# Token-block loads and sink logits as indirect transfers with one row index per partition (one-core hybrid diffusion backbone)

## The chip, the core and the metric

The kernel runs on one core of one Trainium2 chip. A core has the tensor engine (PE in the profile, its weight loads PEld), the vector engine (DVE), the scalar engine (ACT), GpSimd (POOL) and the sync engine (SP), and 16 DMA engines that move data between the device memory and the on-chip memory of 128 partitions. The metric is the device time of one execution in microseconds; of several executions the median is taken.

## What is computed

Two layers run over 768 tokens of width 1024 in float32: 256 context tokens and 512 latent tokens. Cut to what matters here:

```
for l in range(2):
    mod   = silu(c)  @ w_mod[l] + b_mod[l]            # six vectors of shift, scale and gate
    h     = modulate(rms_norm(x, norm_mix_w[l]), mod[0], mod[1])
    mixed = [HGRN2 recurrence, windowed attention with swa_sink[l], neighbourhood attention](h @ w_in[l])
    x     = x + mod[2] * (mixed @ w_out[l])
    h     = modulate(rms_norm(x, norm_ffn_w[l]), mod[3], mod[4])
    q     = h @ peer_wq[l];  scores against 2 x 128 subkeys, top 16 of 16 x 16 per head, 8 heads
    y     = sum over the retrieved experts e of  g_e * gelu(u_e . h) * v_e      # 16384 experts
    x     = x + mod[5] * y
return rms_norm(x_latent, final_norm_w)
```

The context tokens take part in the first layer's feed-forward step and are only read in the second. `swa_sink` has shape (2, 6): one logit for each layer and head, which joins the softmax of the windowed attention.

## The kernel before

The 768 tokens are six blocks of 128 (`NB = 6`, blocks 0 and 1 are context). The residual stream lives between the stages in the device memory, in the tensor `xs` of 768 rows and 1024 columns. The on-chip memory holds a ring of four weight slots of 1 MB, a large `arena` whose places are used anew by each stage, and the pair buffers `hS`, `wS` and `gS_` of the expert products.

SP streams the weights and nothing else: 40 tiles of 1 MB (modulation, input and output projections) for each layer and, for each expert pass, 8 tiles of `wq` and 128 tiles of experts, each 1 MB, into the ring, as slots come free (`stream`, L260).

The work is cut into stages. At the end of each, `stage_end` (L243) lets PE, DVE, ACT and POOL drain, add one to `stage_end` and wait for all four. The stages of a layer are mod, norm, projA, hg, readout, projB, rope, attn, mixT and mix. Then come the expert passes over two blocks each (three in the first layer, two in the second), with the stages pnorm, topk, gbuild, gemm and pres. In gemm all 16384 experts are applied densely to 256 tokens, 128 experts to a step, each product split in high and low parts: PE runs 24 matmuls of 256 columns (L847) and 12 of 512 (L862) in a step.

POOL issues every DMA that isn't a weight stream, in program order:

- At the start (L296 to L298) it loads the constants `ident`, `iota`, `c` and `lb`, and then for each layer the six token blocks (L311) and nine small things (L313 to L319), the sink logits among them: one DMA that repeats the 24 bytes of `swa_sink[l]` over 128 partitions. DVE waits for the four constants (its L1359, before L1360) to compute silu(c); PE's first matmul (L637) waits for that. DVE waits for the nine small loads with `layer_in` at the end of the mod stage.
- At the end of mod (L321, L322) POOL waits for DVE's gates and stores them.
- `load_pass` (L376 to L378) loads the two token blocks of an expert pass from `xs` into `xl`. ACT waits for both in pnorm (L1046) before its first instruction there (L901). For the first pass of a layer it is called at the start of the stage pnorm (L380), with the subkeys behind it (L384). For the others it is called in the gemm stage of the pass before.
- In gemm, POOL waits until all but eight of the 128 expert steps have their gates (`gfull`, L422). Then it issues the gate vector (L425), the two blocks again for the residual (`xr`, L427 and L428), and, where another pass follows, the subkeys (L430) and `load_pass`. DVE needs `gbP` and `xr` in the stage pres (L1706 to L1709), after which POOL stores the two blocks (L436).

POOL computes as well: the bias mask (L348), a product in topk (L397) and the scaled one-hot rows in gbuild (L412, L413).

## Time and profile before

| | |
|---|---|
| three runs | 7344.88, 7344.93 and 7348.73 us, median 7344.93 |
| profiled execution, first to last instruction | 7343.4 us |
| PE, share of the span | 85% (6235.5 us) |
| DVE | 56% (4125.4 us) |
| ACT | 33% (2451.6 us) |
| POOL | 12% (847.7 us) |
| mean granted clock of TensorE | 0.867 |
| DMA | 859.86 MB, mean 117 GB/s |

The profiled execution's own device time isn't given apart from its span. The span is 1.5 us below the median of the runs, and that difference is taken as what lies around it.

The page lists busy time by engine; below it the trace gives instructions in order of time with the idle time before them and what ended it, groups of instructions by line, waits, and the issue and landing of each DMA. For a DMA that POOL issues, the time on the engine is only the issue; "landing" is counted from the start of the issue to the last increment of its semaphore. The granted clock is a share of full speed, 2.4 GHz: 1.00 is that level and 0.50 the other, 1.2 GHz.

### The profile page before, as it was taken

To read this page: it belongs to the slowest core of one execution; us is meant where nothing else is said; L and a number is where in the kernel's file an instruction comes from. 1 tells how busy PE (TensorE), PEld (TensorE's weight loads), DVE (VectorE), ACT (ScalarE), POOL (GpSimd) and SP (SyncE) were. 2 spreads that over 40 slices of the span, in tenths; PEclk is the share of its full clock that TensorE was granted. 3 is DMA by queue.
4 is the path that set the end of the run, shared out by engine and by line. 5 is a ranking of instruction groups with operands and counts; after the bars stand their busy time and mean duration, and the time that the engine had idled before them with its cause. 6 is when DMAs were issued, how large, how long until landed. Compare 5 with 4: busy or idle time off the path is not lost. (4 is left out here: it accounts for less than half of the span.)

```text
span 7343.4 us, 99482 instructions
## 1 busy us (share of the span) xinstructions
PE 6235.5 (85%) x34486; PEld 5371.5 (73%) x34486; DVE 4125.4 (56%) x7294; ACT 2451.6 (33%) x3904; POOL 847.7 (12%) x917
## 2 busy tenths in 40 slices
PE   8659997599995899985999986599858999669997
PEld 3546776499984799974899845468647999559997
DVE  1561335955558755569555515623296555785554
ACT  1111321244441344432444412212114444224444
POOL 0000020600003400006000000001142000060000
PEclk9768558799997999997999997685679999889999
DMA  5001012055551255540455540010213555305554
GB/s 194 18 0 43 9 49 95 0 183 188 185 200 46 87 188 188 184 156 0 177 184 187 197 170 18 6 38 22 81 38 115 188 185 186 129 18 188 188 184 171
DMA packets 127361, 859.86 MB, mean 117 GB/s; under 512 B 15544, under 2 KB 15592, under 8 KB 29320
## 3 DMA queue, kind: packets, MB, share of 16 engines
q1 hardware_dynamic: 109440, 796.97, 29.9%
q0 software_dynamic: 17808, 61.46, 2.4%
q8 instruction: 63, 1.03, 0.1%
q14 instruction: 50, 0.41, 0.0%
HBM read 845.74 MB, written 12.62 MB: 117 GB/s over the span
## 5 line engine op out<-in xcount | busy, mean ns | idle before, releaser
L847 PEld LDWEIGHTS PS<-hS,wS 128*128 128x128 f32 x15360 | 1929.9, 192 | 68.0 <-issue 11.5
L847 PE MATMUL PS<-hS,wS 128*128 128x256 f32 x15360 | 1947.2, 283 | 16.6 <-ACT wS L1085 16.6
L862 PE MATMUL PS<-wS,gS_ 128*128 128x512 f32 x7680 | 1863.1, 391 | 8.7 <-ACT wS L1101 8.7
L862 PEld LDWEIGHTS PS<-wS,gS_ 128*128 128x128 f32 x7680 | 1401.3, 188 | 275.9 <-issue 8.2
L1673 DVE TENSOR_TENSOR wS<-ring,wS 128x1024 fp32r<-128x1024 f32 x640 | 784.0, 1225 | 926.8 <-ACT wS L1085 926.8
L1085 ACT ACTIVATE wS<-ring 128x1024 fp32r<-128x1024 f32 x640 | 678.1, 1060 | 1002.6 <-PE PS L847 1001.7
L1691 DVE TENSOR_TENSOR wS<-ring,wS 128x1024 fp32r<-128x1024 f32 x640 | 784.2, 1225 | 343.5 <-ACT wS L1101 343.5
L1101 ACT ACTIVATE wS<-ring 128x1024 fp32r<-128x1024 f32 x640 | 667.9, 1044 | 7.3 <-PE PS L862 7.3
L1659 DVE TENSOR_TENSOR wS<-iota,arena 128x512 fp32r<-128x512 f32 x640 | 647.2, 1087 | 0.6
L824 PE MATMUL PS<-wS,arena 128*128 128x128 f32 x2560 | 466.7, 340 | 203.9 <-POOL arena L413 198.1
L824 PEld LDWEIGHTS PS<-wS,arena 128*128 128x128 f32 x2560 | 400.0, 239 | 271.4 <-ACT arena L1070 184.4
L1097 ACT ACTIVATE gS_<-arena 128x256 fp32r<-128x256 f32 x640 | 267.3, 418 | 859.3 <-DVE arena L1683 859.3
L413 POOL TENSOR_TENSOR arena<-wS,arena 128x512 f32<-128x512 f32 x320 | 474.0, 1481 | 65.5 <-DVE wS L1659 65.5
L1687 DVE TENSOR_TENSOR gS_<-arena,gS_ 128x256 fp32r<-128x256 f32 x640 | 272.4, 426 | 309.5 <-ACT gS_ L1097 309.5
L425 POOL DMA_DIRECT2D arena<-gates x5 | 3.0, 594 | 3396.5 <-DVE arena L1683 3396.5
L1070 ACT ACTIVATE arena<-PS 128x512 f32 x320 | 191.1, 597 | 596.7 <-PE PS L824 596.7
L793 PE MATMUL PS<-arena,ring 128*128 128x256 f32 x1280 | 303.4, 393 | 44.6 <-DVEq L246 30.7
L793 PEld LDWEIGHTS PS<-arena,ring 128*128 128x128 f32 x1280 | 246.1, 197 | 91.7 <-issue 58.8
L542 PE MATMUL PS<-ring,arena 128*128 128x256 f32 x1152 | 255.6, 384 | 51.6 <-DVEq L246 48.6
L542 PEld LDWEIGHTS PS<-ring,arena 128*128 128x128 f32 x1152 | 220.8, 193 | 86.4 <-DVEq L246 48.9
L584 PE MATMUL PS<-arena 64*128 (+2 forms) x576 | 270.6, 640 | 4.0 <-DVE arena L1180 4.0
L1683 DVE TENSOR_TENSOR arena<-arena 128x256 f32<-128x256 f32 x640 | 267.3, 418 | 5.6 <-ACT arena L1094 5.6
(247 smaller groups left out, 5335.4 us busy)
## 6 DMA issues: line engine op xcount, KB each, us to landing
ring<-in_experts SPq DMA_DIRECT2D x640, 1024.0 KB, 4.8
ring<-in_wcat SPq DMA_DIRECT2D x80, 1024.0 KB, 4.8
ring<-in_wq SPq DMA_DIRECT2D x40, 1024.0 KB, 4.8
arena<-xs POOLq DMA_DIRECT2D x34, 512.0 KB, 6.9
arena<-in_rpb POOLq DMA_DIRECT2D x96, 128.0 KB, 2.6
xs<-arena POOLq DMA_DIRECT2D x20, 512.0 KB, 2.9
arena<-in_subk POOLq DMA_DIRECT2D x5, 1024.0 KB, 11.2
arena<-gates POOLq DMA_DIRECT2D x9, 512.0 KB, 4.7
```

Of the source, the lines that this page charges most:

```text
L413: pool.tensor_tensor(oneA[g % 2], oneR[g].bitcast(F32), arena[:, bass.ds(i * (4 * GD) + (KT0 + 2 * PASS + 4 * g), 4)].unsqueeze(2) .broadc ...
L542: mm = pe.matmul(bank[n % 4][:, 0:TW], hT[:, k, part * P:(part + 1) * P], w[:, k, :], start=(k == 0), stop=(k == KD - 1))
L793: mm = pe.matmul(bank[n % 4][:, 0:PASS], w[:, m, k, :], hP[:, k, :], start=(k == 0), stop=(k == KD - 1))
L824: mm = pe.matmul(bank[4 + g][:, q * P:(q + 1) * P], oneA[g % 2][:, q, :], oneB[g][:, q, :].bitcast(F32), start=True, stop=True)
L847: mm = pe.matmul(bank[c % 2][:, 0:PASS], u[:, k, :], hS[:, h, k, :], start=(part == 0 and k == 0), stop=(part == 2 and k == KD - 1))
L862: mm = pe.matmul(bank[4 + 2 * tb + h], gS_[:, 2 * (c % 2) + g, tb * P:(tb + 1) * P], wS[:, 2 + v, 512 * h:512 * h + 512], start=(start and ...
L1085: act.activation(wS[:, 0, :], ring[:, sl, 0:D], ACT.Copy).then_inc(s["u_hi"], 1)
L1101: act.activation(wS[:, 2, :], ring[:, c, D:2 * D], ACT.Copy).then_inc(s["v_hi"], 1)
L1659: last = dve.tensor_tensor(dst[g], iota[:, :].unsqueeze(1).broadcast_to([P, 4, P]), at.unsqueeze(2).broadcast_to([P, 4, P]), ALU.is_equal)
L1673: dve.tensor_tensor(wS[:, 1, :], ring[:, c % SLOTS, 0:D], wS[:, 0, :].bitcast(F32), ALU.subtract).then_inc(s["u_lo"], 1)
L1687: dve.tensor_tensor(gS_[:, 2 * (c % 2) + 1, :], gel[2 + c % 2], gS_[:, 2 * (c % 2), :].bitcast(F32), ALU.subtract).then_inc(s["gated"], 1)
L1691: dve.tensor_tensor(wS[:, 3, :], ring[:, c, D:2 * D], wS[:, 2, :].bitcast(F32), ALU.subtract).then_inc(s["slot_free"], 1)
```

## The change

A new tensor `rowid` of 18 unsigned words in each partition is filled at the program's start by 18 `iota` instructions on POOL. Column b (0 to 5) holds `b * 128 + partition`, the row of `xs` that belongs to the partition in block b. Columns 6 to 17 hold one number in all partitions, the flat position of one sink logit. POOL waits for all 18 before it goes on.

The loads of `xl` (`load_pass`) and `xr` become indirect transfers (`rows_of`): each partition's row of 4 KB is fetched from the row of `xs` that `rowid` names. That is 20 DMAs, the same bytes to the same places. The one DMA of the sink logits in each layer becomes six, one for each head, each bringing 4 bytes to each of 128 partitions (`sinks_of`); they stand behind the other eight small loads, and the count that DVE waits for rises from 144 to 224 (14 times 16). The loads of `xin`, `xw` and `xf`, all stores, the subkeys and the weights stay as they are.

`rowid` stands ahead of `arena`, which is 32 words shorter. In the built programs `arena` begins 96 bytes later than before, and `hS`, `wS` and `gS_` 32 bytes earlier; the ring and the small tensors ahead of it stay.

```diff
...
         modp = sb("modp", [P, 4 * KD, 2])
         modA = sb("modA", [P, 2, KD, 2])
         small = sb("small", [P, 160])
-        ARENA = 35264
+        rowid = sb("rowid", [P, NB + DEPTH * SWA_H], U32)
+        ARENA = 35232
         arena = sb("arena", [P, ARENA])
 
         hS = sb("hS", [P, 2, KD, PASS], F32R)
...
             "sub_in", "s_done", "s_used", "gexp", "gready", "sel_ready", "selT_done", "one_ready",
             "rows_ready", "eq_want", "eq_done", "u_hi", "u_lo", "v_hi", "h_hi", "gfull", "g_hi", "down_done",
             "one_used", "g_used", "hu_done", "gelu_done", "gated", "fin_ready", "fin_out0", "fin_out1",
-            "nrm_in")}
+            "nrm_in", "ids_ready")}
         w_ready = [sem(f"w_ready{i}") for i in range(SLOTS)]
         block = ctx.enter_context(nc.Block())
         N_STAGED = 4
...
                 pool.dma_start(dst, src).then_inc(s["consts_in"], 16)
 
             pool.nop().then_inc(s["bias_ready"], 1)
+            for b in range(NB):
+                pool.iota(rowid[:, b:b + 1], [[0, 1]], base=b * P, channel_multiplier=1).then_inc(s["ids_ready"], 1)
+            for i in range(DEPTH * SWA_H):
+                pool.iota(rowid[:, NB + i:NB + i + 1], [[0, 1]], base=i, channel_multiplier=0).then_inc(s["ids_ready"], 1)
+            pool.wait_ge(s["ids_ready"], NB + DEPTH * SWA_H)
+
+            def rows_of(dst, b, signal):
+
+                pool.indirect_dma_start(out=dst, out_offset=None, in_=d["xs"][:, :],
+                                        in_offset=bass.IndirectOffsetOnAxis(ap=rowid[:, b:b + 1], axis=0)
+                                        ).then_inc(signal, 16)
+
+            def sinks_of(l):
+
+                flat = d["sink"].rearrange("l (h o) -> (l h) o", o=1)
+                for h in range(SWA_H):
+                    at = NB + l * SWA_H + h
+                    pool.indirect_dma_start(out=sink[:, h:h + 1], out_offset=None, in_=flat,
+                                            in_offset=bass.IndirectOffsetOnAxis(ap=rowid[:, at:at + 1], axis=0)
+                                            ).then_inc(s["layer_in"], 16)
+
             for dst, src in ((ident[:, :], d["ident"]), (iota[:, :], d["iota"]), (c0, d["c"]), (lbx, d["lb"])):
                 const(dst, src)
 
...
 
                 for dst, src in ((bT, d["bT"][l]), (nw, d["nw"][l]),
                                  (brow[0:2, :], d["bgate"][l:l + 1, :].broadcast_to([2, 2048])),
-                                 (sink, d["sink"][l:l + 1, :].broadcast_to([P, SWA_H])),
                                  (arena[:, CST:CST + 512], d["masks"]), (arena[:, CST + 512:CST + 768], d["rope"]),
                                  (arena[:, CST + 768:CST + 1024], d["swam"]), (natm, d["natm"]),
                                  (hnw, d["hnw"][l:l + 1, :].broadcast_to([P, 256]))):
                     pool.dma_start(dst, src).then_inc(s["layer_in"], 16)
+                sinks_of(l)
 
                 pool.wait_ge(s["mod_done"], l + 1)
                 pool.dma_start(d["gates"][l], grow[0:2, :]).then_inc(s["gates_out"], 16)
...
 
                 def load_pass(b0):
                     for i in range(2):
-                        pool.dma_start(xl[:, i, :], d["xs"][(b0 + i) * P:(b0 + i + 1) * P, :]).then_inc(s["xp_in"], 16)
+                        rows_of(xl[:, i, :], b0 + i, s["xp_in"])
 
                 load_pass(passes_of(l)[0])
                 for pn, b0 in enumerate(passes_of(l)):
...
                     pool.dma_start(gbP, d["gates"][l, st:st + 1, D:2 * D].broadcast_to([P, D])
                                    ).then_inc(s["gate_in"], 16)
                     for i in range(2):
-                        pool.dma_start(xr[:, i, :], d["xs"][(b0 + i) * P:(b0 + i + 1) * P, :]).then_inc(s["gate_in"], 16)
+                        rows_of(xr[:, i, :], b0 + i, s["gate_in"])
                     if b0 + 2 < NB:
                         pool.dma_start(subk, d["subk"][l]).then_inc(s["sub_in"], 16)
                         load_pass(b0 + 2)
...
                         dve.tensor_copy(arena[0:2, bass.ds(i * 2048 + (ROWS + 1024 * r), 1024)], PS[r][0:2, :]
                                         ).then_inc(s["row_taken"], 1)
                 dve.wait_ge(s["row_taken"], MOD_TILES // SLOTS * (l + 1) + 2)
-                dve.wait_ge(s["layer_in"], 144 * (l + 1))
+                dve.wait_ge(s["layer_in"], 224 * (l + 1))
 
                 dve.wait_ge(s["modT_done"], l + 1)
                 link(dve.tensor_tensor(modp[:, :, :], bank[4][:, 0:64].rearrange("p (n s) -> p n s", s=2), bT, ALU.add))
```

POOL at the start of the program, before (from the branch into the engine's block to the first token loads):

```order
L287 UNCONDITIONAL_BRANCH
L293 DMA ident<-in_ident 128x128
L293 DMA iota<-in_iota 128x128
L293 DMA small<-in_c 128x16
L293 DMA small<-in_lb 128x8
L311 DMA arena<-in_ctx 128x1024 x2
L311 DMA arena<-in_x 128x1024 x4
```

and now:

```order
L288 UNCONDITIONAL_BRANCH
L298 ISA
L298 IOTA rowid 128x1 x6
L300 IOTA rowid 128x1 x12
L294 DMA ident<-in_ident 128x128
L294 DMA iota<-in_iota 128x128
L294 DMA small<-in_c 128x16
L294 DMA small<-in_lb 128x8
L333 DMA arena<-in_ctx 128x1024 x2
L333 DMA arena<-in_x 128x1024 x4
```

The ISA row stands for the reload of POOL's instruction library and the 18 iotas for the row numbers; both now stand ahead of the four constants. Before, the reload stood ahead of the first mask sum in the stage attn (L348).

POOL from the stage mix to the first product of topk in the first layer, before:

```order
L370 DMA xs<-arena 128x1024 x6
L378 DMA arena<-xs 128x1024 x2
L384 DMA arena<-in_subk 128x2048
L397 TENSOR_TENSOR arena<-arena 128x1024 x6
L413 TENSOR_TENSOR arena<-wS,arena 128x512 x2
```

and now:

```order
L392 DMA xs<-arena 128x1024 x6
L305 DMA arena<-xs,rowid 128x1024 x2
L406 DMA arena<-in_subk 128x2048
L419 TENSOR_TENSOR arena<-arena 128x1024 x6
L435 TENSOR_TENSOR arena<-wS,arena 128x512 x2
```

The two block loads stand at the same place, ahead of the subkeys, and read `rowid` besides `xs`.

POOL at the end of the first expert pass (gemm and pres), before:

```order
L425 DMA arena<-gates 128x1024
L428 DMA arena<-xs 128x1024 x2
L430 DMA arena<-in_subk 128x2048
L378 DMA arena<-xs 128x1024 x2
L436 DMA xs<-arena 128x1024 x2
```

and now:

```order
L447 DMA arena<-gates 128x1024
L305 DMA arena<-xs,rowid 128x1024 x2
L452 DMA arena<-in_subk 128x2048
L305 DMA arena<-xs,rowid 128x1024 x2
L458 DMA xs<-arena 128x1024 x2
```

Four of the six loads are indirect now; their order is the same.

## Rows read from the trace of the kernel before

**Rows 1.** The page: the span, and from its part 5 the costliest matmul groups.
```profile
span 7343.4 us, 99482 instructions
...
L847 PE MATMUL PS<-hS,wS 128*128 128x256 f32 x15360 | 1947.2, 283 | 16.6 <-ACT wS L1085 16.6
L862 PE MATMUL PS<-wS,gS_ 128*128 128x512 f32 x7680 | 1863.1, 391 | 8.7 <-ACT wS L1101 8.7
```

**Rows 2.** Instructions in order of time, POOL, 0 to 60 us: start, us, engine line op [idle before].
```profile
0.38 0.10 POOL L1809 MEMSET const-float32-0.0<- 128x1 f32 x1 [0.38 <-issue]
0.42 0.10 POOL L1809 MEMSET const-float32-1.0<- 128x1 f32 x1
...
3.25 0.53 POOL L293 DMA_DIRECT2D small<-in_lb  x1
```

**Rows 3.** The same, DVE, 0 to 175 us.
```profile
9.85 0.21 DVE L1360 TENSOR_SCALAR sT<-small 128x16 f32<-128x16 f32 x1 [9.85 <-DMA small<-in_lb]
...
42.44 1.21 DVE L1381 COPY arena<-PS 2x1024 f32 x1 [12.60 <-PE PS L637]
56.26 1.21 DVE L1381 COPY arena<-PS 2x1024 f32 x1 [12.61 <-PE PS L637]
...
101.23 0.23 DVE L1387 TENSOR_TENSOR modp<-PS,small 128x64 f32<-128x64 f32 x1 [2.33 <-PE PS L644]
```

**Rows 4.** The same, PE, 0 to 175 us.
```profile
12.63 84.91 PE L637 MATMUL PS<-ring,sT 128*2 128x256 f32 x384 [12.63 <-DVEq L1373]
```

**Rows 5.** Groups of instructions of POOL: mean ns after the busy time.
```profile
L412 POOL TENSOR_TENSOR small<-small 128x1 f32<-128x1 f32 x310 | 138.3, 446 | 49.3 <-POOL arena L413 15.3 <-PE PS L824 5.6 <-DVE wS L1659 3.1
L397 POOL TENSOR_TENSOR arena<-arena 128x1024 f32<-128x1024 f32 x30 | 80.6, 2712 | 609.0 <-DVE arena L1297 609.0
...
L378 POOL DMA_DIRECT2D arena<-xs x10 | 5.3, 530 | 20.1 <-POOLq L246 20.1
```

**Rows 6.** Line L348, 700 to 712 us: counts, ns min/median/max, start.
```profile
L348 POOLq MODIFY_POOL_CONFIG  x2: 42/42/42, 708.2 to 708.3; - x2
L348 POOL TENSOR_TENSOR arena<-arena x1: 1254/1254/1254, 710.3 to 710.3; 128x512 f32<-128x512 f32 x1
```

**Rows 7.** Instructions in order of time, POOL, 480 to 760 us.
```profile
710.31 1.25 POOL L348 TENSOR_TENSOR arena<-arena 128x512 f32<-128x512 f32 x1 [2.06 <-DMA arena<-in_rpb]
...
714.71 1.25 POOL L348 TENSOR_TENSOR arena<-arena 128x512 f32<-128x512 f32 x1 [2.14 <-DMA arena<-in_rpb]
```

**Rows 8.** The same, POOL, 1160 to 1205 us.
```profile
1173.74 1.06 POOL L378 DMA_DIRECT2D arena<-xs  x2 [10.15 <-POOLq L246]
```

**Rows 9.** The same, ACT, 1160 to 1205 us.
```profile
1179.79 1.06 ACT L901 ACTIVATE arena<-arena 128x1024 f32<-128x1024 f32 x1 [104.15 <-DMA arena<-xs]
```

**Rows 10.** The same, POOL, 5272 to 5300 us.
```profile
5282.55 1.06 POOL L378 DMA_DIRECT2D arena<-xs  x2 [9.94 <-POOLq L246]
```

**Rows 11.** The same, ACT, 5272 to 5300 us.
```profile
5288.20 1.06 ACT L901 ACTIVATE arena<-arena 128x1024 f32<-128x1024 f32 x1 [77.20 <-DMA arena<-xs]
```

**Rows 12.** Landing of the ten loads of L378 in us.
```profile
DMA to landing us min/median/max: 3.9/14.0/15.3
```

**Rows 13.** DMA, 1173 to 1176 us: queues, MB, share of the 16 engines.
```profile
q1 hardware_dynamic: 144, 0.98, 77.7%
```

**Rows 14.** Instructions in order of time, POOL, 2137 to 2195 us.
```profile
2138.14 0.59 POOL L425 DMA_DIRECT2D arena<-gates  x1 [680.37 <-DVE arena L1683]
2138.72 1.05 POOL L428 DMA_DIRECT2D arena<-xs  x2
...
2140.28 1.05 POOL L378 DMA_DIRECT2D arena<-xs  x2
```

**Rows 15.** Landing of the ten loads of L428 in us.
```profile
DMA to landing us min/median/max: 5.3/6.3/7.7
```

**Rows 16.** Instructions in order of time, DVE, 2183 to 2215 us.
```profile
2186.78 1.22 DVE L1708 TENSOR_TENSOR arena<-PS,arena 128x1024 f32<-128x1024 f32 x1 [1.98 <-ACTq L246]
```

**Rows 17.** Waits of POOL: us in total, times, longest us.
```profile
POOL gates L322 <- DVE arena L1393: 178.0, 2, 93.3
```

## The prediction, made before the changed kernel ran

> **What bounds the kernel now.** I read the page first, then, for each place that the change touches, the instructions in order of time on POOL and on the engine that waits for it, then the landings of POOL's DMAs. The page gives a span of 7343.4 us and the two matmul groups of the expert steps, 1947.2 and 1863.1 us busy: these 3810 us are the body of the kernel, and nothing of the change stands in a step [rows 1]. So the change can act only where somebody waits for POOL or for one of its loads, or where it slows somebody at a distance. The trace shows three kinds of such places.
>
> The start: POOL issues the four constants from 1.5 us, and the last, `lb`, is issued at 3.25 us [rows 2]. DVE's first instruction waits for it until 9.85 us [rows 3], and PE's first matmul follows at 12.63 us and then runs for 84.91 us without a pause [rows 4]. DVE takes a result every 13.82 us (56.26 less 42.44), and had waited for PE all the time between: PE sets the pace of this stage, the weights are there [rows 3]. A later start of PE is a later end of the stage, one for one.
>
> The first pass of each layer: POOL issues the two loads of `xl` at 1173.74 us and ACT starts at 1179.79 us, 6.05 us later [rows 8, 9]. In the second layer it is 5282.55 to 5288.20, 5.65 us [rows 10, 11]. Every engine stands still meanwhile.
>
> The last eight steps of a gemm: POOL starts to issue at 2138.14 us and DVE wants the first of it at 2186.78 us. That is 48.64 us of cover [rows 14, 16].
>
> **The 18 iotas at the start: 4.4 us, on the path.** No iota is in the trace. Below, it can't be less than the spacing of two memsets of the same shape, 0.04 us (0.42 less 0.38): 18 x 0.04 = 0.7 us [rows 2]. Above, I take POOL's 128x1 sum, 446 ns, which reads two operands that an iota hasn't: 18 x 0.446 = 8.0 us [rows 5]. An iota writes one column as the memset does, but its function has to be called as the sum's is. I take the middle, 0.245 us: 18 x 0.245 = 4.4 us. The wait for all 18 stands behind them in the same queue; I give it 0.1 us, an allowance.
>
> **The library reload: 1.0 us, on the path.** The change moves the reload of POOL's library from the attention to the start. Before, two pool configurations stand at 708.2 us and the product after them starts at 710.31, 2.1 us after the first [rows 6]. It waited 2.06 us there for a DMA, and the next such product, with no reload ahead of it, waited 2.14 [rows 7]. So the reload was hidden and costs between 0 and 2.1 us; I take the middle, 1.0. At the start nothing hides it, since `lb`'s load is behind it. Nothing comes back in the attention, where the DMA is waited for anyway.
>
> The Trainium skill, "GPSIMD Engine Reference", section Instruction dispatch, has it otherwise: the first call to freshly loaded code pays about 6 us that no instruction shows. The row doesn't agree, since the product ran 2.1 us after the configurations; by the page the sum would be 5.0 us higher, and the verdict the same.
>
> `lb`'s own landing, 6.6 us after its issue today (9.85 less 3.25), was already beside the ring's stream, and I leave it [rows 2, 3]. Together the start costs 4.4 + 0.1 + 1.0 = 5.5 us, between 0.7 and 10.2 (8.0 + 0.1 + 2.1).
>
> **The sinks: nothing.** Five more DMAs in each layer, and six of them indirect, stand last among the small loads. Behind them POOL waits for DVE's gates, 178.0 us in two waits, so up to 93.3 and at least 84.7 us [rows 17]. Even at 7 us each, six take 42. DVE needs all of them only at 101.23 us [rows 3]. The cover is gone at 14 us each.
>
> **The indirect issue itself.** Call x the time that POOL needs to issue one load of 128 rows by index. The direct one takes 0.530 us [rows 5]. An indirect one does the same and reads 128 numbers besides, so it can't be less. Above, the longest group of POOL instructions has a mean of 2.712 us [rows 5]. Nearest is a direct issue plus one small reading instruction: 0.530 + 0.446 = 0.98 us. I take x = 1.0.
>
> **The first pass of each layer: 1.0 us in all.** The fastest of the ten loads of this line landed 3.9 us after its issue began, 3.4 after it ended [rows 12]. Two indirect issues in a row and one such landing give 2x + 3.4: at x = 1.0 that is 5.4 us, less than the 6.05 and 5.65 of now, because now both compete with the ring, whose stream held 77.7% of the DMA engines' work in the first 3 us [rows 13]. So part of the longer issue lies beside traffic that was awaited anyway. I count half of the added issue, 0.5 us a layer, 1.0 us in all. At x = 2.712 the formula gives 8.8 us: 2.8 and 3.2 more, 6.0 together. The lower end is nothing. The subkeys are issued 1 us later and aren't needed before topk.
>
> The Trainium skill, "DMA: Bandwidth & Descriptors", section Anatomy of one DMA, calls descriptor generation "small, variable" beside a fixed 2.0 us for a transfer. By that x would stay at 0.53 and this term would be 0; the 3.4 us above, with 512 KB to move, don't speak against it.
>
> **The gemm stages: nothing.** There are 20 indirect loads, and 16 of them are issued here. In the three passes that another follows in their layer, four stand behind the gate vector and beside the subkeys: 4x + 0.59 + 0.53 = 5.1 us of issue against 48.64 us of cover [rows 14, 16]. `xr`'s own landing, 7.7 us at most today, stands inside it too [rows 15]. In the last pass of a layer there are two. What is queued behind them on POOL is only the end of the stage. The cover is gone at x = (48.64 - 1.12) / 4 = 11.9 us. The bytes and the rows of 4 KB are the same, so the ring sees what it sees now.
>
> **The sum.** 5.5 + 1.0 = 6.5 us: a span of 7349.9 us. The profiled execution's span lies 1.5 us below the median of the runs, 7344.93; so the time is 7351.4 us, 0.09% more. The bounds of the terms give 0.7 to 16.2 us more, 7345.6 to 7361.1. A measurement of this kernel can tell about 0.2%, 14.7 us, from no change.
>
> **The rivals.**
>
> *POOL walks the index list (slower).* The rows of a DMA are shared by 16 engines. If POOL reads the indices for each of them by a step of its own, at the price of its smallest reading instruction, x = 16 x 0.446 = 7.1 us [rows 5]. The first passes then take 2 x 7.1 + 3.4 = 17.6 us instead of 6.05 and 5.65: 11.55 + 11.95 = 23.5 us. With the start that is 29 us more: 7374 us. The gemms still hide it (28.4 + 1.1 = 29.5 us). It decides from x = 3.6 on: 2 x 3.6 + 3.4 = 10.6 in each of two layers is 21.2, less the 11.7 of now 9.5, and 9.5 + 5.5 passes 14.7. For it: nothing in this trace reads a list on POOL. Against it: a direct load writes entries for the same 128 rows in 0.53 us [rows 5]. I give it 15 in 100.
>
> The Trainium skill's "GPSIMD Engine Reference", section Performance pitfalls for Q7 kernels, has a rule of this kind: about 102 cycles for each read command, "e.g. one per gather index", that don't overlap. With 128 in a row at the 1.2 GHz of its specifications this is an estimate of 10.9 us for x, and 7389 us. No row here shows such reads.
>
> *The layout (either sign).* `hS`, `wS` and `gS_` start 32 bytes earlier, `arena` 96 later. If an engine or a DMA depends on where in a line of memory a row starts, all 640 steps feel it: 0.4% of 3810 us is 15 us [rows 1]. For it: these four are nearly all that the steps touch. Against it: no row compares two placements. 7366 or 7336 us; 3 in 100 on each side.
>
> *A shorter way (faster).* The rows of an indirect load may be given to the DMA engines otherwise and land sooner. All of the wait that it could take away is 6.05 + 5.65 = 11.7 us less the issue, so this alone can't pass 0.2%. Only together with another granted clock after one of the waits could it. I give 2 in 100, at 7328 us.
>
> *It does nothing:* if x = 0.53 and an iota costs as a memset, 0.7 us more. This is the lower end of my forecast, not a case of its own.
>
> **How the numbers follow.** Forecast 0.77, walk 0.15, layout 0.06, shorter way 0.02. The bounds of the forecast reach over 14.7 us at their end (16.2), for which I move 0.02 to slower. Faster: 0.03 + 0.02 = 0.05. Slower: 0.15 + 0.03 + 0.02 = 0.20. Within 0.2%: 0.75. The likeliest case gives 7351.4 us. The range begins at 7343.0, somewhat below the lower bound, and ends at 7376, so that the walk as priced is held; outside are the layout, the shorter way, a walk at a longer step and some of the forecast's own error.
>
> **What would show it.** POOL's rows at the start: 18 iotas of about 0.25 us and `lb` issued near 8.8 us instead of 3.25; PE's first matmul near 18.1 instead of 12.63 us, and the mod stage later by the same. The indirect loads near 1.0 us of issue each, and 6 to 7 us from the first of them to ACT in the first passes. In gemm, ACT, DVE and PE keep their steps while POOL issues, and the stage pres waits for nothing of POOL's. I am wrong if `lb`'s landing doesn't delay PE, if an indirect issue takes over 3.6 us, or if L847 and L862 (now under other line numbers) change their means.

## The result and the profile after

| | before | after |
|---|---|---|
| runs of the comparison | 18 | 18 |
| median, us | 7346.11 | 7361.57 |
| lowest and highest, us | 7340.90, 7349.15 | 7355.06, 7369.85 |
| profiled execution, span, us | 7343.4 | 7358.8 |
| mean granted clock of TensorE | 0.867 | 0.865 |

The ratio is 1.0022 with a 95% interval of 1.0015 to 1.0029: 15.5 us slower. That is a difference, and a hair over the 0.2% that I called the edge of what can be told. The time is within the range of the prediction (7343.0 to 7376.0), but 9 us of the 15.5 are not in its sum. Three executions of the later comparisons took 13574, 18489 and 27077 us at a granted clock far from the others' 0.866; they move a median by 0.4 us at most and are left out of the ratios.

The page of after, the lines that answer to [rows 1]:

```profile
span 7358.8 us, 99500 instructions
PE 6240.5 (85%) x34486; PEld 5375.6 (73%) x34486; DVE 4126.8 (56%) x7294; ACT 2453.8 (33%) x3904; POOL 872.7 (12%) x945
L869 PE MATMUL PS<-hS,wS 128*128 128x256 f32 x15360 | 1947.5, 283 | 16.6 <-ACT wS L1107 16.6
L884 PE MATMUL PS<-wS,gS_ 128*128 128x512 f32 x7680 | 1863.2, 391 | 8.7 <-ACT wS L1123 8.7
```

The body of the kernel is as it was: 1947.5 and 1863.2 us against 1947.2 and 1863.1. So the time came in at the edges, and I followed them in order. POOL at the start, which answers to [rows 2] (start, duration, engine, line, operation):

```profile
1.06 0.50 POOL L298 IOTA rowid<- 128x1 uint32 x6 [0.47 <-POOLq L1831]
1.52 0.94 POOL L300 IOTA rowid<- 128x1 uint32 x12
2.77 0.70 POOL L294 DMA_DIRECT2D ident<-in_ident  x1 [0.31 <-POOL rowid L300]
...
4.54 0.53 POOL L294 DMA_DIRECT2D small<-in_lb  x1
...
12.77 1.03 POOL L314 DMA_INDIRECT small<-in_sink,rowid  x1 [0.30 <-issue]
14.11 0.98 POOL L314 DMA_INDIRECT small<-in_sink,rowid  x1 [0.30 <-issue]
...
19.13 0.94 POOL L314 DMA_INDIRECT small<-in_sink,rowid  x1 [0.30 <-issue]
```

All 18 iotas take 1.40 us (2.46 less 1.06), and `lb` is issued at 4.54 instead of 3.25 us. The six sink loads are issued by 20.07 us. PE in order of time, 0 to 180 us and 4205 to 4345 us, which answers to [rows 4]:

```profile
13.44 18.84 PE L659 MATMUL PS<-ring,sT 128*2 128x256 f32 x80 [13.44 <-DVEq L1395]
35.94 67.46 PE L659 MATMUL PS<-ring,sT 128*2 128x256 f32 x304 [3.65 <-DMA ring<-in_wcat]
...
4230.75 26.52 PE L659 MATMUL PS<-ring,sT 128*2 128x256 f32 x112 [9.32 <-ACTq L247]
4260.91 58.87 PE L659 MATMUL PS<-ring,sT 128*2 128x256 f32 x272 [3.64 <-DMA ring<-in_wcat]
```

Here is what I hadn't foreseen. PE ran 384 matmuls without a pause in [rows 4]. Now it stands still in both layers, for 3.65 and 3.64 us, and what it waits for is no load of POOL's but a weight tile of the ring (16 matmuls use one up). The DMA view of 20 to 34 us, in 40 slices of 0.35 us (busy tenths of the DMA engines, then GB/s), first before the change and then after it:

```profile
DMA  9999225899999999999998999999999999999998
GB/s 410 404 329 49 82 105 176 339 410 468 439 421 421 456 369 386 392 375 416 468 410 374 445 398 421 445 398 468 421 398 421 398 421 445 468 421 398 351 398 351
```

```profile
DMA  9999999989899989111101001003432275585789
GB/s 374 410 387 281 363 375 416 380 322 415 351 445 369 381 328 352 59 59 47 25 0 47 24 24 24 24 23 95 164 141 117 117 258 234 211 304 234 304 351 398
```

From 25.6 us on, traffic falls from some 400 to between 0 and 59 GB/s for about 3.9 us (11 slices) and takes another 4 us to come back. The digits are as low: the DMA engines are busy for less than a fifth of each slice. Before the change there was a small hollow of the same kind, four slices long, near 21 us. The weight tiles of the ring come in through the same stretch. Their number, size and median time to landing there, before and after:

```profile
ring<-in_wcat SPq DMA_DIRECT2D x4, 1024.0 KB, 7.1
```

```profile
ring<-in_wcat SPq DMA_DIRECT2D x4, 1024.0 KB, 12.3
```

The mod stage ends later by the wait and a little more. The granted clock in windows of PE from 28.90 us on (columns: us, PE busy and matmuls, clock as a share of 2.4 GHz, DMA share, GB/s):

```profile
28.90:32.28 3.38, 3.38 (x16) 1.00 0.38 148
32.28:35.94 3.66, 0.01 (x2) 1.00 0.87 360
35.94:37.94 2.00, 2.00 (x7) 0.72 1.00 422
37.94:39.94 2.00, 2.00 (x6) 0.50 0.97 406
39.94:41.94 2.00, 2.00 (x11) 0.93 0.61 258
```

After 3.66 us of standing still the clock falls to its lower level (0.50 is 1.2 GHz) for some 3 us. There eight matmuls start 0.427 us apart instead of 0.216, which costs 1.7 us. The stage begins with such a slow stretch in every kernel, 7 to 13 matmuls long; here it is seven, before it was nine, which gives 0.4 us back. All 384 matmuls take 86.30 us (18.84 + 67.46) instead of 84.91 [rows 4]. So the stage ends 0.81 (PE's start, 13.44 less 12.63) + 3.65 + 1.39 = 5.85 us late; DVE's row at its end, at 101.23 us in [rows 3], reads:

```profile
107.10 0.23 DVE L1409 TENSOR_TENSOR modp<-PS,small 128x64 f32<-128x64 f32 x1 [2.34 <-PE PS L666]
```

107.10 less 101.23 is 5.87 us. In the second layer the stage grows by 3.6 us once more. There the wait is as long, and no slow stretch follows it:

```profile
4260.91:4319.78 58.87, 58.87 (x272) 1.00 0.85 309
```

The first passes, POOL and ACT in order of time, and then the group of all twenty indirect block loads with their landing. They answer to [rows 8 to 12]:

```profile
1181.57 1.00 POOL L305 DMA_INDIRECT arena<-xs,rowid  x1 [10.32 <-POOLq L247]
1182.88 0.97 POOL L305 DMA_INDIRECT arena<-xs,rowid  x1 [0.30 <-issue]
```

```profile
1188.56 1.06 ACT L923 ACTIVATE arena<-arena 128x1024 f32<-128x1024 f32 x1 [104.34 <-DMA arena<-xs,rowid]
...
5299.17 1.06 ACT L923 ACTIVATE arena<-arena 128x1024 f32<-128x1024 f32 x1 [76.79 <-DMA arena<-xs,rowid]
```

```profile
L305 POOL DMA_INDIRECT arena<-xs,rowid x20: 937/968/2060, 1181.6 to 7275.5; - x20
...
DMA to landing us min/median/max: 3.9/8.2/14.8
```

ACT starts 6.99 us after the first issue in layer 1 (before: 6.05) and 6.07 us after it in layer 2 (5293.10; before: 5.65). An issue takes 0.97 us.

A table of how much later than before each mark comes, in us, in the profiled executions of after and of three experiments, shows where the difference grows. The last column is the end:

| | end of mod 1 | first pass 1 | end of layer 1 | end of mod 2 | first pass 2 | last gemm starts | end |
|---|---|---|---|---|---|---|---|
| after | 5.87 | 8.77 | 7.01 | 10.73 | 10.97 | 14.14 | 15.4 |
| sinks direct | 2.10 | 3.52 | 3.25 | 3.19 | 2.60 | 3.45 | 4.7 |
| blocks direct | 5.68 | 6.74 | 6.95 | 9.48 | 7.89 | 10.11 | 10.0 |
| iotas only | 1.64 | -0.57 | -2.50 | -3.34 | -3.91 | -0.26 | 1.8 |

Steps of 1 to 4 us also stand between marks where nothing was changed: a single execution can't tell less than that. The medians have to.

### The profile page after: what moved, and what is told of

The parts are those of the page before. It is cut to its first block and busy times, and to the rows that moved or that the text cites. A ratio compares the mean times of both kernels' runs of the same rounds, so it can differ in the third digit from the quotient of the medians.

```text
span 7358.8 us, 99500 instructions
## 1 busy us (share of the span) xinstructions
PE 6240.5 (85%) x34486; PEld 5375.6 (73%) x34486; DVE 4126.8 (56%) x7294; ACT 2453.8 (33%) x3904; POOL 872.7 (12%) x945
## 3 DMA queue, kind: packets, MB, share of 16 engines
q8 instruction: 63, 1.03, 0.1%
## 5 line engine op out<-in xcount | busy, mean ns | idle before, releaser
L869 PE MATMUL PS<-hS,wS 128*128 128x256 f32 x15360 | 1947.5, 283 | 16.6 <-ACT wS L1107 16.6
L884 PE MATMUL PS<-wS,gS_ 128*128 128x512 f32 x7680 | 1863.2, 391 | 8.7 <-ACT wS L1123 8.7
L564 PE MATMUL PS<-ring,arena 128*128 128x256 f32 x1152 | 255.7, 384 | 51.6 <-DVEq L247 48.6
```

The costliest lines, as they stand in the source:

```text
L564: mm = pe.matmul(bank[n % 4][:, 0:TW], hT[:, k, part * P:(part + 1) * P], w[:, k, :], start=(k == 0), stop=(k == KD - 1))
L869: mm = pe.matmul(bank[c % 2][:, 0:PASS], u[:, k, :], hS[:, h, k, :], start=(part == 0 and k == 0), stop=(part == 2 and k == KD - 1))
L884: mm = pe.matmul(bank[4 + 2 * tb + h], gS_[:, 2 * (c % 2) + g, tb * P:(tb + 1) * P], wS[:, 2 + v, 512 * h:512 * h + 512], start=(start and ...
```

## The experiments

Twelve runs were made, of eleven kernels (11 is the kernel of 8). The theories carry letters in the expectations: A, the sink loads hold up the ring, with A1, because a table of twelve rows is spread over too few DMA engines; P, because there are so many small pieces; and R, because all pieces read one address (P and R together are A2 in the first expectations, and Q is the width of a piece). B: the block loads cost it. C: the later start. D: the layout. All diffs are against the changed kernel unless said otherwise.

**1. Sinks as one direct load again, all else as changed.**

```
                                  (brow[0:2, :], d["bgate"][l:l + 1, :].broadcast_to([2, 2048])),
+                                 (sink, d["sink"][l:l + 1, :].broadcast_to([P, SWA_H])),
...
-                sinks_of(l)
...
-                dve.wait_ge(s["layer_in"], 224 * (l + 1))
+                dve.wait_ge(s["layer_in"], 144 * (l + 1))
```

> The change with the sinks loaded as before, one direct DMA a layer at its old place; iotas and the 20 indirect block loads stay. Theory A (the sinks' small indirect transfers hold back a weight tile in each mod stage, 5.5 us of drift in the first layer and 3.8 in the second): PE shows no wait for a tile in either mod stage, the end of mod lies within 1.5 us of before plus the start's 0.8, and the time is 5 to 7 us over before, some 9 us under the change. Rival B (the block loads cost the time, by their longer issue and later landing in the first pass of each layer and at the gemm ends): 12 to 15 us over before remain. Rival C (the later start alone shifts the weight stream against the token loads and makes the stall): the stall is still there.

Measured: 7351.26 us against 7346.68 before, ratio 1.0007 (0.9998 to 1.0016). PE in order of time:

```profile
13.99 85.64 PE L659 MATMUL PS<-ring,sT 128*2 128x256 f32 x384 [13.99 <-DVEq L1395]
...
4227.17 85.08 PE L659 MATMUL PS<-ring,sT 128*2 128x256 f32 x384 [9.49 <-ACTq L247]
```

The wait is gone in both layers, and with it some two thirds of the loss (15.5 less 4.6 us by the medians).

**2. Block loads direct again, sinks still indirect.**

```
-                        rows_of(xl[:, i, :], b0 + i, s["xp_in"])
+                        pool.dma_start(xl[:, i, :], d["xs"][(b0 + i) * P:(b0 + i + 1) * P, :]).then_inc(s["xp_in"], 16)
...
-                        rows_of(xr[:, i, :], b0 + i, s["gate_in"])
+                        pool.dma_start(xr[:, i, :], d["xs"][(b0 + i) * P:(b0 + i + 1) * P, :]).then_inc(s["gate_in"], 16)
```

> The change with xl and xr loaded directly as before; the iotas and the twelve indirect sink loads stay. Theory A: both stalls of PE for a weight tile stay, 9 to 10 us over before. Rival B: under 4 us over before. If the two parts add up, this difference and that of the run with direct sinks sum to the 15.5 us of the change plus about 1 us for the iotas, counted twice.

Measured: 7355.46 us, 8.8 more than before, ratio 1.0014 (1.0005 to 1.0023). PE:

```profile
13.53 18.75 PE L659 MATMUL PS<-ring,sT 128*2 128x256 f32 x80 [13.53 <-DVEq L1395]
35.75 67.46 PE L659 MATMUL PS<-ring,sT 128*2 128x256 f32 x304 [3.48 <-DMA ring<-in_wcat]
```

The wait belongs to the sinks, not to the blocks.

**3. The sinks' table padded from 12 to 16 rows.** The Trainium skill, "DMA: Bandwidth & Descriptors", section "Why a DMA increments its semaphore by 16 and not by 1", states that a DMA uses the largest number of engines up to 16 that divides the outer sizes of both sides. By that a table of 12 rows and a tile of 128 partitions would go over 4 engines, one of 16 rows over all 16, if the rule holds for the table of an indirect load.

```
-                flat = d["sink"].rearrange("l (h o) -> (l h) o", o=1)
+                flat = d["sink"]
...
-    A["sink"], A["hnw"] = a["swa_sink"], a["hgrn_norm_w"]
+    A["sink"], A["hnw"] = np.concatenate([a["swa_sink"].reshape(12, 1), np.zeros((4, 1), np.float32)]), a["hgrn_norm_w"]
```

> The change with the table of sink logits padded from 12 to 16 rows, four of them zero and never read; same indices, same 768 packets of 4 bytes a layer. Theory A1 (the number of rows of the source, 12, lets only 4 of the 16 DMA engines carry the sinks, as 4 is the largest number up to 16 that divides 12 and 128; those four hold back their share of a weight tile): with 16 rows all 16 engines share the packets, 8 each instead of 32 for a DMA, and the stall falls to a quarter or less: under 1.5 us in each mod stage, 6 to 8 us over before. Rival A2 (what counts is the total of small packets or that all read one address): the stall stays at 3.7 us of PE's wait and more.

Measured: 7358.38 us against 7346.68, ratio 1.0015 (1.0006 to 1.0025). PE:

```profile
31.04 3.61 PE L659 MATMUL PS<-ring,sT 128*2 128x256 f32 x16 [1.92 <-DMA ring<-in_wcat]
35.38 65.77 PE L659 MATMUL PS<-ring,sT 128*2 128x256 f32 x304 [0.72 <-DMA ring<-in_wcat]
...
4257.22 58.87 PE L659 MATMUL PS<-ring,sT 128*2 128x256 f32 x272 [2.93 <-DMA ring<-in_wcat]
```

5.6 us of waiting instead of 7.3. The wait shrinks and stays: the number of rows is at most a part of it. The trace doesn't name the engine of a packet, so no run here shows the rule, and on how many engines either table went stays open. In both kernels, and in 8 and 9, a layer's six sink loads show 96 packets of 32 bytes, eight pieces in each.

**4. Six direct loads of 4 bytes, repeated over the partitions, in place of the six indirect ones.**

```
-                    pool.indirect_dma_start(out=sink[:, h:h + 1], out_offset=None, in_=flat,
...
+                    pool.dma_start(sink[:, h:h + 1], flat[at - NB:at - NB + 1, :].broadcast_to([P, 1])).then_inc(s["layer_in"], 16)
```

> The change with each of the six sink loads of a layer as a direct DMA that repeats one 4-byte logit over 128 partitions; the same number of DMAs and packets, no index. Theory A1 (few engines because of the 12-row source): a direct DMA is spread over all 16 engines, the stall is gone, 5 to 8 us over before. Rival A2 (small packets or one address as such): the stall stays. The issue falls from 0.94 to about 0.54 us each.

Measured: one run, 7360.4 us, span 7358.1. PE, and the DMA view of 20 to 34 us:

```profile
32.64 70.92 PE L657 MATMUL PS<-ring,sT 128*2 128x256 f32 x320 [2.21 <-DMA ring<-in_wcat]
```

```profile
DMA  9999999940000000001111223569999999999999
GB/s 433 410 406 285 351 375 357 311 107 12 0 1 0 0 1 24 24 24 47 47 47 47 94 71 117 211 258 375 421 445 445 398 421 445 421 421 445 445 398 421
```

The wait is there without any index, in layer 2 too (3.34 us), and so is the hollow in the traffic. It begins earlier, as the loads are issued earlier (0.57 us each). What stalls the ring isn't the indirect transfer as such: the change had replaced one small load by six.

**5. Only the iotas and the layout: no indirect load at all.** The edits of experiments 1 and 2 together.

> The change without any indirect transfer: only rowid, its 18 iotas and the wait for them at the start; block loads and sinks as before. What it costs is the later start alone: PE's first matmul 0.8 to 1.4 us later (13.44 and 13.99 us were seen against 12.63), the end of mod 1 to 2 us later, no wait of PE for a weight tile. Theory A: 1 to 3 us over before. Rival C (the shift of the start makes the stalls): 8 us and more. Rival D (the 32 and 96 bytes by which the buffers moved cost in every expert step): 3 us and more, growing evenly over the passes.

Measured: 7346.79 us against 7345.12, ratio 1.0001 (0.9992 to 1.0010), PE without a pause (13.41 us, 384 matmuls in 85.76 us). The later start makes no stall, so C falls. The time alone, with an interval of -6 to 7 us, can't exclude the 3 us of D. The matmul groups speak against it: that of 256 columns took 1949.0 us here and 1949.5 in experiment 12, which has the old layout. The medians are 1.7 us apart.

**6. The six sink loads issued after the mod stage.**

```
                 end(f"mod{l}")
+                sinks_of(l)
                 end(f"norm{l}")
...
-                dve.wait_ge(s["layer_in"], 224 * (l + 1))
+                dve.wait_ge(s["layer_in"], 224 * l + 128)
...
                 end(f"rope{l}")
+                dve.wait_ge(s["layer_in"], 224 * (l + 1))
```

> The change with the twelve indirect sink loads issued one stage later, after the stage mod, while the norm stage runs and the ring is full; DVE waits for them only ahead of the attention. Theory A (it is the meeting of the small packets with a weight stream that PE awaits at once): no wait of PE for a tile in the mod stages, and the time falls to that of the run with direct sinks, 7351 us, plus at most 1. Rival (the sinks cost wherever they stand): a wait for a tile at the start of projA, 7356 us or more.

Measured: 7348.10 us against 7345.12, ratio 1.0006 (0.9997 to 1.0015). The sinks go out at 110.48 to 117.8 us, when the ring's stream stands still (2 GB/s of traffic from 104 to 132 us), and nobody waits. PE in the mod stage:

```profile
13.34 85.15 PE L659 MATMUL PS<-ring,sT 128*2 128x256 f32 x384 [13.34 <-DVEq L1395]
```

The same loads cost nothing that shows in a stretch that doesn't live from the ring tile by tile. With experiment 11 it is the cheapest form of the change that keeps both kinds of indirect load.

**7. Six direct loads of 24 bytes.** As experiment 4, but each brings the whole row of six logits, five of the six into columns of their own that nobody reads. For these `arena` is 64 words shorter.

```
...
+                    dst = sink if h == 5 else sinkx[:, (5 * l + h) * SWA_H:(5 * l + h + 1) * SWA_H]
+                    pool.dma_start(dst, d["sink"][l:l + 1, :].broadcast_to([P, SWA_H])).then_inc(s["layer_in"], 16)
```

> The change with the six sink loads of a layer as direct DMAs that each bring all 24 bytes of the layer's logits to each of the 128 partitions, five of them to a scratch tensor that nobody reads: 768 packets as in the change and as in the run with six direct 4-byte DMAs, but six times as wide. Theory P (what holds the weight tile back is the number of small packets): PE waits for a tile as with six direct DMAs of 4 bytes, 2.2 us in the first layer. Rival Q (it is the width of 4 bytes): no wait.

Measured: one run, 7366.4 us. PE waits 3.82 us for a tile in layer 1 and 3.15 us in layer 2:

```profile
33.80 69.23 PE L659 MATMUL PS<-ring,sT 128*2 128x256 f32 x320 [3.82 <-DMA ring<-in_wcat]
```

The width of a piece isn't the cause: this is the very load of before, six times.

**8. Still 768 indirect pieces of 4 bytes, but each partition reads a row of its own.** The table is written out to 1536 rows.

```
-                pool.iota(rowid[:, NB + i:NB + i + 1], [[0, 1]], base=i, channel_multiplier=0).then_inc(s["ids_ready"], 1)
+                pool.iota(rowid[:, NB + i:NB + i + 1], [[0, 1]], base=i * P, channel_multiplier=1).then_inc(s["ids_ready"], 1)
...
+    A["sink"], A["hnw"] = np.concatenate([np.repeat(a["swa_sink"].reshape(12), P).reshape(1536, 1), np.zeros((1536-1536, 1), np.float32)]), a["hgrn_norm_w"]
```

> The change with a table of sink logits of 1536 rows, each logit repeated 128 times, so that every partition reads a row of its own; 768 packets of 4 bytes as before, 16 DMA engines (1536 and 128 are both divisible by 16). Theory P (number of small packets): the wait stays as with the table of 16 rows, 2.6 us in the first layer. Rival R (all 128 reads of a DMA go to one address and queue there): the stall goes, under 0.5 us.

Measured: one run, 7349.65 us, span 7347.9. PE, and the DMA view of 20 to 34 us:

```profile
13.47 85.79 PE L659 MATMUL PS<-ring,sT 128*2 128x256 f32 x384 [13.47 <-DVEq L1395]
```

```profile
DMA  9998999966367799999999999999999694599999
GB/s 398 458 387 284 335 381 351 340 135 95 119 237 282 282 446 398 421 398 421 445 421 398 421 445 398 445 445 375 398 398 538 281 304 187 234 375 421 421 445 421
```

This is the run that decides. As many loads, as many pieces, as small, issued at the same time by the same instructions: only the addresses (and the size of the table) differ, and PE doesn't wait, in layer 2 neither. P falls, R stands. The six logits of the change lie side by side in 24 bytes and the 768 of this table in 3 KB, so whether one word or a small piece of memory is what can't be read so often at once stays open.

**9. The same with a table of 1540 rows, which 16 doesn't divide.** The diff is that of experiment 8 with `1540-1536` for `1536-1536`; by the rule of experiment 3 it would go over 4 engines.

> As the run with a table row of its own for each partition, but the table has 1540 rows, of which the last four are never read: the largest number up to 16 that divides 1540 and 128 is 4. Packets, indices and addresses are those of that run. Theory R (one address) alone: no wait of PE for a tile, as there, 7349 to 7352 us. If few engines add to it on their own: a wait of 1 us and more in the first mod stage. That also tells what made the stall smaller with the table of 16 rows than in the change.

Measured: one run, 7355.29 us, span 7353.1. PE doesn't wait in either mod stage (384 matmuls in 84.74 and in 85.36 us), and the first ends 1.19 us late, against 1.72 in experiment 8. Of its other time 3.5 us come between the norm and the end of the HGRN stage (2.09 us late before, 5.57 after), where no load of the change stands: there the first 64 matmuls of projA took 22.95 us instead of 20.91. It is a single run, so what caused this stays open. If this table goes over fewer engines, that doesn't stall PE without the common address.

**10. One indirect load a layer, of a row of 24 bytes, the same row for all.**

```
...
+                pool.indirect_dma_start(out=sink, out_offset=None, in_=d["sink"][:, :],
+                                        in_offset=bass.IndirectOffsetOnAxis(ap=rowid[:, NB + l:NB + l + 1], axis=0)
+                                        ).then_inc(s["layer_in"], 16)
...
-                dve.wait_ge(s["layer_in"], 224 * (l + 1))
+                dve.wait_ge(s["layer_in"], 144 * (l + 1))
```

> The change with one indirect DMA of the sinks for each layer, whose row is the layer's six logits (24 bytes), the same row for all 128 partitions: 128 packets at one address instead of 768. Theory R with the dose as the number of reads of one address: a sixth of the stall, so under 1 us of PE's wait, and likely none, since the ring has tiles in hand; 7349 to 7353 us. Rival (an indirect DMA with equal indices is slow in itself): PE waits for a tile, 7355 us or more.

Measured: one run, 7352.33 us, span 7350.1, and no wait:

```profile
13.56 85.11 PE L656 MATMUL PS<-ring,sT 128*2 128x256 f32 x384 [13.56 <-DVEq L1392]
```

128 reads of one place are too few to empty the ring; 768 are enough.

**11. The kernel of experiment 8 again, several executions.**

> The kernel of the run with a table row for each partition once more, now timed in rounds. Theory R: the change without its stalls, 4 to 5 us over before, as with direct sinks (7351.3 against 7346.7 us), and 9 to 11 us under the change (7361.6).

Measured: 7350.71 us against 7347.36, ratio 1.0006 (0.9997 to 1.0015), no wait of PE. With distinct addresses the six indirect loads cost no more that can be told than leaving them out (experiment 1: 1.0007).

**12. The kernel before, with both findings turned to use.** The sinks come from a table of 128 rows, one for each partition, in one direct load, so that even the 128 reads of one address are gone; and `c` and `lb` are loaded ahead of the other constants, with a semaphore of their own. The diff is against the kernel before.

```
-            for dst, src in ((ident[:, :], d["ident"]), (iota[:, :], d["iota"]), (c0, d["c"]), (lbx, d["lb"])):
+            for dst, src in ((c0, d["c"]), (lbx, d["lb"])):
+                const(dst, src, "c_in")
+            for dst, src in ((ident[:, :], d["ident"]), (iota[:, :], d["iota"])):
...
-                                 (sink, d["sink"][l:l + 1, :].broadcast_to([P, SWA_H])),
+                                 (sink, d["sink"][l]),
...
-    A["sink"], A["hnw"] = a["swa_sink"], a["hgrn_norm_w"]
+    A["sink"], A["hnw"] = np.repeat(a["swa_sink"][:, None, :], P, axis=1), a["hgrn_norm_w"]
```

> The kernel before with two things that the experiments point to and no part of the change: the constants c and lb are loaded first, with a semaphore of their own, so that DVE's first instruction waits for them alone; and the sink logits come from a table with a row for each partition (128 x 6 a layer), read by one direct DMA instead of one that reads the same 24 bytes 128 times. lb is issued 1.2 us earlier, so PE's first matmul stands near 11.4 instead of 12.63 us and the mod stage ends 1.2 us earlier. The quiet stretch of the DMA engines in the kernel before, 49 to 176 GB/s between 21 and 22.5 us, shortens or goes if the sinks' reads of one address make it, and stays if it belongs to the other repeated reads there (hnw, bgate). The time: 1 us under before, which a comparison in rounds can't tell from none.

Measured: 7344.33 us against 7346.02, ratio 0.9999 (0.9990 to 1.0008). PE in order of time, and the traffic of 20 to 34 us:

```profile
10.99 85.72 PE L638 MATMUL PS<-ring,sT 128*2 128x256 f32 x384 [10.99 <-DVEq L1376]
```

```profile
GB/s 398 404 351 319 269 469 352 421 421 351 456 410 375 339 451 410 375 392 339 433 404 380 468 410 433 445 421 374 421 468 398 421 421 445 421 421 375 445 398 351
```

PE starts 1.64 us earlier (12.63 less 10.99) and takes 0.81 us longer for its 384 matmuls, as 13 of them instead of 9 stand 0.427 us apart in the slow stretch at the start; 0.8 us is left at the end of the stage. The hollow of 49 to 176 GB/s is gone. Two things were changed here, and the view alone can't say which of them took it away; the packets below point to the sinks. Together the effects are too small to be told in the time: no version that beats both kernels was found.

**The packets of the sinks in layer 1.** The trace has every DMA packet with its size, its start and the time that it took. 128 pieces of 24 bytes show as 16 packets of 192 bytes, 768 pieces of 4 bytes as 96 packets of 32. Where the sinks are loaded after the stage (experiment 6), none of either size stands there.

| | packets | first to last start, us | median and longest, ns |
|---|---|---|---|
| before: 128 reads of one place | 16 of 192 bytes | 20.82 to 21.39 | 1159, 1374 |
| 12: a row for each partition | 16 of 192 bytes | 20.78 to 22.19 | 15, 15 |
| 7: 768 reads of one place | 96 of 192 bytes | 22.62 to 30.31 | 908, 1881 |
| after: 768 reads of six words | 96 of 32 bytes | 23.85 to 35.27 | 15, 15 |
| 8: 768 words | 96 of 32 bytes | 22.62 to 25.21 | 13, 15 |
| 11: 768 words | 96 of 32 bytes | 22.83 to 26.10 | 13, 15 |

The same 16 packets take some 1.2 us each where all read one place and 0.015 us where each partition has its own. The packets of 32 bytes are short in every kernel, but with common words the 96 are spread over 11.4 us, with words of their own over 2.6 and 3.3. In layer 2 the difference is smaller: 13.0 us against 7.0 and 9.8.

## Why the prediction was right and where it was wrong

**The body: right.** The two matmul groups moved by 0.3 and 0.1 us, so the layout rival, priced at 15 us, fell; experiment 5 has the layout without any indirect load and lies 1.7 us over before by the medians.

**The iotas: mis-sized.** I had 4.4 us from half of POOL's 128x1 sum. An iota of this shape shows 121 ns and the next starts some 75 ns after it, so they overlap: 1.4 us for 18, each half of what I had foretold. The lower bound, the spacing of memsets (0.7), was nearer.

**The library reload: mis-sized.** I had 1.0 us. The two pool configurations stand at 0.97 and 1.00 us and the first iota at 1.06: less than 0.1 us. The whole start, `lb`'s issue, is 1.29 us late; `lb` lands 6.00 us after its issue (10.54 less 4.54) instead of 6.60, and 0.81 reaches PE, whose first matmul stands at 13.44 and not near 18.1 us. The Trainium skill, "GPSIMD Engine Reference", section Instruction dispatch, would have put about 6 us there. The trace doesn't agree: within the span no such time is seen, and nothing was added ahead of it either, since device time less span is 1.9 us on average, with the change and without. Together the start was 0.8 us of PE's time in the profile of after (0.7 to 1.4 over all kernels with iotas) where I had 5.5.

**"The sinks: nothing": this step failed.** Its arithmetic on POOL was right: six issues of 0.94 to 1.03 us with 0.30 between them, all landed 16.5 us after issue at the latest, over 65 us before DVE needs them. But I asked only whether the loads come in time for their own reader and how long POOL is busy. I didn't ask what they do to others on the 16 DMA engines, in a stage in which PE uses up a 1 MB tile every 3.5 us (84.91 / 24) and the whole traffic of some 400 GB/s, if it were all the ring's, would bring one in 2.6 (an estimate). The runs show the answer in three moves: the wait goes with the sinks (1) and not with the blocks (2), it doesn't need the index (4, 7), and it goes when the same number of pieces reads different addresses (8, 11). In the profile of after it is 3.65 + 3.64 us of waiting and 1.39 us by which the first stage's matmuls took longer (the lower clock behind the wait, less the shorter slow stretch at the start), 8.7 us in all. The medians put it at 7 to 11 us, each difference with an interval of 5 to 7 us on either side: with the sinks restored the loss falls from 15.5 to 4.6 us, 10.9 less; with the sinks as the only indirect loads it is 8.8 us, against 1.7 for the iotas alone, 7.1 more. That many reads of one place are slow is seen twice, in 8 against the rest and in single packets (1159 against 15 ns, before against 12). Why they are slow isn't visible: the records don't show what the memory does.

**The indirect issue: right.** x = 1.0 forecast, 0.94 to 1.00 measured, with 0.30 us before the next, and 2.04 for the first of each group in gemm. POOL doesn't walk the index list 16 times: this rival (x = 7.1, and an estimated 10.9 by the Trainium skill's "GPSIMD Engine Reference", section Performance pitfalls for Q7 kernels) fell at once. The Trainium skill's "DMA: Bandwidth & Descriptors", section Anatomy of one DMA, which was weighed there too, would have left x at the direct 0.53; the rows show 0.97, so the index has a price of about 0.4 us and a further 0.3 us of gap.

**The first passes: mis-sized.** I counted half of the added issue, since the rest would lie beside traffic awaited anyway. It doesn't. Two indirect issues end 2.28 us after the first began (1183.85 less 1181.57), two direct ones 1.06: 1.22 us more in each layer, 2.4 in both. From first issue to ACT, the four traces with direct loads show means of 5.76 and 5.65 us in layers 1 and 2, the ten with indirect ones 7.18 and 6.61: 1.42 + 0.96 = 2.4 us. So by these means the whole added issue stood on the path; the term was 1.0, and the trace of after alone has 1.4.

**The gemm stages: right.** POOL in order of time at the end of the first pass, which answers to [rows 14]:

```profile
2145.75 2.04 POOL L305 DMA_INDIRECT arena<-xs,rowid  x1 [0.31 <-issue]
...
2151.21 0.94 POOL L305 DMA_INDIRECT arena<-xs,rowid  x1 [0.30 <-issue]
2196.50 0.57 POOL L458 DMA_DIRECT2D xs<-arena  x1 [44.35 <-DVE arena L1731]
```

The issue, 7.3 us from 2144.82 (the gate vector) to 2152.15, lies inside the 48.6 us of cover.

**The sum.** Forecast 5.5 + 1.0 = 6.5 us. In the profile of after: start 0.8, the ring's tiles 8.7, first passes 1.4 (0.94 + 0.42), together 10.9 of the 15.4. The other 4.5 us are steps of 1 to 3 us where nothing was changed. One is seen at the start of the last gemm, where PE's clock in its first 4.8 us is 0.64 after and 1.00 before, and the first 24 matmuls take 4.51 us instead of 3.10. Twelve of the fourteen traces have this step, experiment 12 among them, which arrives there 2.9 us earlier than before; only before and experiment 2 lack it. So later arrival isn't needed for it. At the third gemm even the equal kernels 8 and 11 differ by it. Why the clock falls in one and not in the other stays open. The chance of 0.75 for no difference was too high for one reason: it rested on a sum without the ring. The size, 7361.6, lies just beyond the bounds of the sum's own terms (7361.1) and in the range because the walk rival had stretched it. That the range held was luck: none of its terms was the ring's wait.

## What to carry to other kernels

When a change adds loads, check three covers and not two: the issuing engine's, the reader's, and that of every other stream on the same DMA engines; in a stage that eats tiles as they arrive, small loads can cost more than they move. A value repeated over the partitions is better stored repeated, or fetched once, than read many times from one address, and if it must be, in a stage that doesn't live from the stream. An indirect issue costs about twice a direct one here (0.97 against 0.53 us, and 0.30 more before the next); that counts whole where engines stand and wait for it, and nothing under a long gemm.

## What the runs showed that I had not expected

- 768 reads of 4 bytes from six addresses, 3 KB in all, took the traffic from some 400 to at most 59 GB/s for 3.9 us, the ring's with it. Before, 128 reads of one address stood beside a hollow of 1.4 us (49 to 176 GB/s), which was gone in experiment 12. 768 reads of 768 addresses left one of 2.1 us (95 to 282 GB/s, experiment 8), which in experiment 11 went down to 12 GB/s for a slice. Even with no sink load in the stretch one slice fell to 123 GB/s (experiment 6). So it is the length of a hollow and not its depth that tells the kernels apart.
- An idle of 3.66 us in PE was followed by a stretch at the lower clock, which added 1.7 us to a wait of 3.65. The idle's length doesn't decide it: a wait of 2.21 us had such a stretch behind it (experiment 4, clock 0.72 in the 6 us after), waits of 3.64 (after, layer 2) and 3.82 us (experiment 7, layer 1) had none, at a clock of 1.00.
- The first indirect load after a gate vector took 2.04 us to issue, the later ones 0.94 to 0.97; some direct issues near the iotas and the indirect loads took 0.57 us instead of 0.54. Neither matters here.
- Direct loads of 24 bytes are as harmful as of 4 (experiment 7: 3.82 and 3.15 us of waiting): what counts is how often one place is read, not how much.
- One packet of 192 bytes took up to 1.4 us where 128 partitions read one place, and 0.015 us where each had its own (before and experiment 12).
